# Attention in pairs of heads: scores on two row halves, weights normalised before the transpose, sums with features first, three weight buffers

## What is computed

```python
def gqa_attend(q, k, v, scale):
    s = jnp.einsum('bqhgd,bkhd->bhgqk', q, k, preferred_element_type=jnp.float32) * scale
    p = jax.nn.softmax(s, axis=-1)
    return jnp.einsum('bhgqk,bkhd->bqhgd', p.astype(v.dtype), v)
```

## Time and profile before

| | |
|---|---|
| median of 3 runs | 2904.19 us (2891.95 to 2906.38) |
| profiled execution | 2906.38 us, of it 2906.3 from first to last instruction |
| TensorE busy | 2460.7 us (85%) |
| VectorE busy | 1459.9 us (50%) |
| GpSimd busy | 934.2 us (32%) |
| ScalarE busy | 841.4 us (29%) |
| mean granted TensorE clock | 0.915 of full |

### The profile page before, as it was taken

One profiled execution on the slowest core, in us unless ns is written; L12 is line 12 of the kernel. 1 busy time (PEld: TensorE's weight loads), 2 busy tenths in 40 slices (PEclk: granted clock), 3 DMA queues, 4 the chain that ended last, 5 costly groups with the idle time before them and its releaser, 6 DMA issues. The chain is left out here.

```text
span 2906.3 us, 32667 instructions
## 1 busy us (share of the span) xinstructions
PE 2460.7 (85%) x12562; PEld 2053.4 (71%) x12562; DVE 1459.9 (50%) x2490; ACT 841.4 (29%) x1544; POOL 934.2 (32%) x572
## 2 busy tenths in 40 slices
PE   2888667988675988999689999999598997799997
PEld 2777355777354866668479998989487776588886
DVE  4776644876635956447752342222588665300112
ACT  2215113215113155443232121211412443322222
POOL 1431225320235210001354242433652001555554
PEclk9999768988777999899789999999799999899999
DMA  6540012530021310002322232332260000133222
GB/s 227 169 147 8 0 59 90 163 110 1 0 87 48 122 52 1 1 1 79 114 66 95 84 105 80 102 91 69 78 194 29 1 1 22 59 101 95 94 94 73
DMA packets 141906, 218.97 MB, mean 75 GB/s; under 512 B 12148, under 2 KB 64916, under 8 KB 141624
## 3 DMA queue, kind: packets, MB, share of 16 engines
q1 hardware_dynamic: 141752, 216.88, 23.4%
HBM read 214.75 MB, written 2.10 MB: 75 GB/s over the span
## 5 line engine op out<-in xcount | busy, mean ns | idle before, releaser
L284 POOL TENSOR_TENSOR w_lo<-w_raw,w_hi 128x1024 fp32r<-128x1024 f32 (+3 forms) x252 | 591.3, 2347 | 1306.0 <-ACT w_hi L277 1306.0
L277 ACT ACTIVATE w_hi<-w_raw 128x1024 fp32r<-128x1024 f32 (+3 forms) x252 | 255.4, 1017 | 1222.1 <-PE ps L297 986.6
L295 PE MATMUL ps<-w_hi,h_transposed 128*128 128x512 f32 (+3 forms) x1088 | 416.8, 383 | 44.2 <-DVE proj_one L678 20.8
L296 PE MATMUL ps<-w_lo,h_transposed 128*128 128x512 f32 (+3 forms) x1088 | 408.4, 375 | 0.0
L297 PE MATMUL ps<-w_hi,h_transposed 128*128 128x512 f32 (+3 forms) x1088 | 408.0, 375 | 0.0
L295 PE MATMUL ps<-h_transposed,w_hi 128*128 128x384 f32 (+1 forms) x1056 | 373.7, 354 | 3.6 <-issue 2.1
L296 PE MATMUL ps<-h_transposed,w_hi 128*128 128x384 f32 (+1 forms) x1056 | 373.2, 353 | 0.0
L297 PE MATMUL ps<-h_transposed,w_lo 128*128 128x384 f32 (+1 forms) x1056 | 373.1, 353 | 0.0
L355 DVE SCALAR_TENSOR_TENSOR mod_acc_aux<-w_raw,c_act,mod_acc_aux 128x512 f32<-128x512 f32 x280 | 275.4, 1008 | 46.4 <-DMA w_raw<-in_w_mod_dram 24.9
L295 PEld LDWEIGHTS ps<-w_hi,h_transposed 128*128 128x128 f32 x1088 | 212.7, 195 | 85.9 <-POOL w_lo L284 24.1
L1141 DVE TENSOR_TENSOR ffn_full<-ps,ffn_silu 128x768 f32<-128x768 f32 (+1 forms) x44 | 34.2, 819 | 423.6 <-PE ps L297 423.6
(11 more groups left out here) (297 smaller groups left out, 3847.8 us busy)
## 6 DMA issues: line engine op xcount, KB each, us to landing
w_raw<-in_ada_w_dram SPq DMA_DIRECT2D x96, 512.0 KB, 4.2
w_raw<-in_ffn_w_in_dram SPq DMA_DIRECT2D x88, 512.0 KB, 3.6
w_raw<-in_w_mod_dram SPq DMA_DIRECT2D x48, 512.0 KB, 4.6
w_raw<-in_ffn_w_out_dram SPq DMA_DIRECT2D x44, 512.0 KB, 3.6
w_raw<-in_w_in_dram SPq DMA_DIRECT2D x40, 512.0 KB, 4.6
w_raw<-in_w_out_dram SPq DMA_DIRECT2D x16, 512.0 KB, 4.4
w_raw<-in_od_w_in_dram SPq DMA_DIRECT2D x16, 512.0 KB, 4.6
mod_gain<-in_norm_g_dram SPq DMA_DIRECT2D x16, 256.0 KB, 4.1
```

Source lines behind the costliest of these rows:

```text
L277: act.activation(w_hi[:, i % 2, 0:k * n], w_raw[:, u % 4, 0:k * n], ACT.Copy).then_inc(w_hi_ready.sem, 1)
L284: pool.tensor_tensor(w_lo[:, i % 2, 0:k * n], w_raw[:, u % 4, 0:k * n], w_hi[:, i % 2, 0:k * n].bitcast(F32), ALU.subtract).then_inc(w_lo_ ...
L295: pe.matmul(acc, left[0], right[0], start=start, stop=False)
L296: pe.matmul(acc, left[0], right[1], start=False, stop=False)
```

## The change

Attention goes through steps, each a pair of heads.

- **Scores on two row halves.** The keys of one head lie on rows 0 to 63 and again on rows 64 to 127, with no zero halves. Each head's scores are a 64-row matmul on its half; the two heads alternate, piece by piece of the keys. The latent heads have 96 rows and stay on the whole array. The scale is now put into the queries when they are turned.
- **Weights normalised first.** VectorE forms the reciprocals right after the exponentials, and GpSimd multiplies both heads' exponentials by them in place (two TENSOR_SCALAR, L990) before TensorE transposes them. In layer one and the windowed stage GpSimd also adds the sink to the negated maximum (L982), ahead of the multiply of the step before.
- **Sums, features first.** The values are the stationary operand (64 columns) and the transposed weights move. The two heads write the two column halves of the array. The output has features on the partitions; finishing is a copy, or in layer one a product with the gate, which is now turned as well. Joined (differential) steps keep tokens first and scale at the end.
- **Transposes in rounds of four** into PSUM bank 7, a third round into bank 6, which the sums use too. Scores hold six banks. The copies are divided by round.
- **Buffers.** Three weight tiles of two heads in layer one, the windowed and the odd stage (lag 2); two in the latent stages (lag 1).
- **MixTransposed** takes parts that have features first from SBUF and transposes only the rest: nothing in the even layer, half in the others.

```diff
-            self.held, self.lag = (4, 4) if max(len(un["values"]) for un in units) <= 4 else (2, 2)
+            self.wide = max(self.blocks) > 4
+            self.slots = 3 if self.wide else 6
+            self.lag = len(probs) - 1
...
-                        for b, v in enumerate(vals):
-                            ins = pe.matmul(ps[:, 6 + o % 2, 0:v.shape[1]], self.probs_t[:, o % 2, b * P:(b + 1) * P], v,
-                                            start=(b == 0), stop=(b == len(vals) - 1))
...
+                for k in runs:
...
+                    for i in range(2):
+                        sc = self.scores(2 * s + i, w)
+                        done.append(pe.matmul(sc[:, c:c + m], x["q"][i], x["keys"][i][k][0], start=True, stop=not masks))
...
+                for b, v in enumerate(x["values"]):
+                    if self.has_join[s]:
+                        ins = pe.matmul(ps[:, self.SUM_BANK, 0:P], probs_t[:, b * P:(b + 1) * P], v, start=(b == 0), stop=(b == nb - 1))
+                    else:
+                        for i in range(2):
+                            ins = pe.matmul(ps[64 * i:64 * i + 64, self.SUM_BANK, 0:P], v[i], probs_t[:, (i * nb + b) * P:(i * nb + b + 1) * P],
+                                            start=(b == 0), stop=(b == nb - 1))
...
+                n = len(self.steps)
+                for loop in range(n + self.lag + 1):
+                    t, v = loop - self.lag, loop - self.lag - 1
+                    if loop < n:
+                        self.score(pe, loop)
+                    if 0 <= t < n:
+                        self.turn(pe, t, 0)
+                    if 0 <= v < n:
+                        self.sum(pe, v)
+                    if 0 <= t < n:
+                        for r in range(1, len(self.rounds[t])):
+                            self.turn(pe, t, r)
...
+                    s = loop - 1
+                    if s >= 0 and not self.has_join[s]:
+                        w, probs = self.width(s), self.probs[s % len(self.probs)]
+                        self.wait(pool, s_inv, s + 1)
+                        for i in range(2):
+                            r = (2 * s + i) % 16
+                            p = probs[:, i * w:(i + 1) * w]
+                            pool.tensor_scalar(p, p, st[:, 5, r:r + 1], None, ALU.mult).then_inc(s_norm.sem, 1)
...
+                self.groups = [(kt, range(tiles)) for kt in range(len(ready))]
+                self.groups += [(kt, kind) for kt in range(len(ready), KT) for kind in kinds]
```

More of the change, by code:

```diff
@@ L757, in wait_probs_ready @@
[L757 to L768, removed]
+                n = len(steps)
@@ new lines, in __init__ @@
+                self.b[s_norm], self.b[s_joined] = s_norm.plan(2 * plain), s_joined.plan(joined)
+                self.order = [sum(j == k for k in self.has_join[:s]) for s, j in enumerate(self.has_join)]
+                turned = [nb if j else 2 * nb for nb, j in zip(self.blocks, self.has_join)]
+                self.rounds = [[(i, min(4, m - i)) for i in range(0, m, 4)] for m in turned]
+                self.turn0 = [sum(len(r) for r in self.rounds[:s]) for s in range(n + 1)]
+                self.b[s_turned] = s_turned.plan(self.turn0[n])
@@ new lines, in maximum @@
+            def maximum(self, dve, s, heads):
+                u, w, m = 2 * s + heads[0], self.width(s), len(heads)
+                r = u % 16
+                self.wait(dve, s_scored, u + m)
+                if m == 2:
+                    b = u % 6
+                    src, dst = ps[:, b:b + 2, 0:w], self.st[:, 0, r:r + 2]
+                else:
+                    src, dst = self.scores(u, w), self.st[:, 0, r:r + 1]
+                ins = dve.tensor_reduce(dst, src, AX, ALU.max, negate=True)
+                sink = self.steps[s]["sink"]
+                if sink is not None:
+                    dve_s.chain(ins)
+                    h = sink + heads[0]
+                    ins = dve.tensor_tensor(dst, dst, self.neg_sinks[:, h:h + m], ALU.min)
+                ins.then_inc(s_max.sem, m)
@@ new lines, in vector @@
+            def vector(self, dve):
+                n = len(self.steps)
+                for loop in range(n + self.lag + 1):
+                    s, t, v = loop, loop - self.lag, loop - self.lag - 1
+                    if self.lag == 1 and 1 <= s <= n:
+                        self.inverse(dve, s - 1)
+                    if s < n:
+                        for heads in ([[0], [1]] if self.wide else [[0, 1]]):
+                            self.maximum(dve, s, heads)
+                    if 0 <= v < n:
+                        self.finish(dve, v)
+                    if self.lag == 2 and 1 <= s <= n:
+                        self.inverse(dve, s - 1)
+                    if 0 <= t < n:
+                        for r in range(len(self.rounds[t])):
+                            self.keep(dve, s_kept_v, t, r)
@@ L1872, in layer_even @@
-                schedule.append(Attention(units, probsb, probsb_t, stats))
-            schedule.append(MixTransposed(lambda t, kt: PE_[:, t, kt * P:(kt + 1) * P], XT + CT))
+                    blocks = list(range(XT + CT)) if t < XT else [XT, XT + 1]
+                    spans = ((0, S), (S, CTX)) if t < XT else ((S, CTX),)
+                    for j in range(2):
+                        heads = (4 * four + 2 * j, 4 * four + 2 * j + 1)
+                        steps.append(dict(q=[qbT[:, h % 4, tok(t)] for h in heads],
+                                          keys=[[(kbT[:, h % 4, c0:c0 + n], c0 if t < XT else 0) for c0, n in spans] for h in heads],
+                                          masks=[], values=[[vb[:, b, h * 64:h * 64 + 64] for h in heads] for b in blocks], sink=None, kind="plain",
+                                          dst=PE_[:, t, HALF + heads[0] * 64:HALF + heads[0] * 64 + P]))
```

469 lines of the change are left out of this document (251 added, 218 removed).

## The result

The changed kernel takes 2991.85 us (median of 4 runs, 2984.52 to 2994.54) against 2901.18 for the kernel before beside it: ratio 1.031, 95% interval 1.029 to 1.034. It is slower by 3.1%; 2836 had been forecast, and the range ended at 2885. The profiled execution has a span of 2987.5 us, 81.2 more than before.

The account below looks back on a forecast made before the run. TensorE's work was taken to set the odd stage's pace. Odd -60, windowed -19, latent 0, layer one +8 and the rest +3 gave -68: 2906.4 to 2838 profiled, 2836 as median; range 2780 to 2885.

Parts of the forecast that it names:

- The halves of the array: TensorE: two 64-row or 64-column matmuls on different halves run at once, full overlap assumed at 2.4 GHz.
- S: TensorE: price of one change of tiling, read as at most 0.19 us at half clock, taken as 0.10.
- a rival: Scores on row halves: halves keep strict order, the last pass sticks out 0.43 us per 768-wide pair; 2856, chance 0.08.
- Odd layer, -60: Odd attention stage: 8.2 us instead of 12.04 for two steps, 137 us against 197.6.
- I take 1.2: GpSimd's 768-wide multiply: 1.2 us, from 0.51 for a one-column TENSOR_SCALAR plus the fill's 0.69.
- Latent attention, 0: Both latent stages: 768-wide pairs save 8 us, 256-wide context pairs cost 7, start and end 1; no net change.
- Even layer, windowed, -19: Windowed stage: 640-wide steps save 13 us, 512-wide 10, context pairs nothing; longer start and end cost 4.
- Layer one, +4 each: Layer one's two attention stages: 47 us each against 42.6, with 2.7 us for each of 12 steps.
- Some 4.9 us over two steps, 2.4 each: Layer one: chain from exponential through reciprocal, multiplies, transposes, copy and back, spread over two steps.
- The rest, +3: Outside the attention stages: turned gates cost 2 us in each layer, MixTransposed gives -1 in all.
- The rival of dear tiling changes: Some 350 tiling changes at S = 0.40 add 105 us, so the kernel ends slower: 2941, chance 0.04.
- the first rival: Everything at TensorE's pace, multiply near the fill's price, S near 0: odd -68, windowed -27; 2779, chance 0.17.

Follow-up runs that it names:

- the VectorE run: Changed kernel with a plain step's two multiplies moved from GpSimd to VectorE, right behind the reciprocal: 2879.12 us, ratio 0.991 to the kernel before.
- The swap of two calls: Changed kernel with VectorE computing a step's reciprocals before finishing an older step, in three-buffer stages: 2932.77 us, ratio 1.009 to the kernel before.
- The edit that takes the operations apart: Changed kernel with ScalarE making MixTransposed's first four feature high parts before those of the first weights: 2982.77 us, ratio 1.027 to the kernel before.
- the short one: Changed kernel with each GpSimd multiply scaling one column only, all waits kept: 2871.12 us, ratio 0.988 to the kernel before.

## Why the prediction was wrong

Against the forecast of the profiled execution (2838) the change is 149 us late. By its own steps:

- **"The halves of the array": right.** Scores and sums of a pair overlap at 2.4 GHz. A change of tiling: in the windowed ring above the four transposes start at 1170.33 and the sums at 1170.91, 0.14 more than four passes of 0.11. The sums of the odd stage, twelve passes on each half, give the same in the VectorE run: 1.46 us to the next transposes (2327.56 to 2329.02), 0.15 more than 12 of 0.109. S is about 0.15, not 0.10: some 350 x 0.05 = 17 us where all of it is on the path. The rule of the Trainium skill that a rival rested on (TensorE: Matmul & The Clock Gate, Part 3, strict order in the queue) does not hold here: the odd scores, head by head, show passes of a free half running ahead of queued ones of the other, 1.57 us for what takes 1.56 in turns.
- **"Odd layer, -60": mis-sized, -34.** The text had "at 2.12 about 158"; with 2.20 it was 163. The failed term is "I take 1.2" for the multiply. Both of its parts were off: one column takes 0.28 us, not 0.51, and the other 767 take 1.92, not 0.69. With VectorE's 0.62 the stage is 143.5, against 137 forecast for a GpSimd at 1.2; about 5 of the 6.5 left is S (96 x 0.05).
- **"Latent attention, 0": mis-sized, +35 for both.** The same term. The ring of 6.8 us stood in the rival; it measured 6.9. With the multiply on VectorE the two stages take 66.7 and 68.5 us, against 67.9 before.
- **"Even layer, windowed, -19": the bound was wrong, +8.** The step took TensorE's work as the pace and gave GpSimd no place in it. GpSimd alone had 3.1 us a step at 512 columns, and the ring made it 4.0. With either cause taken out the stage still has 95 to 100 us for the 87 forecast; S gives 6 of it (112 x 0.05), and the rest is open.
- **"Layer one, +4 each": +28.6 and +26.6.** "Some 4.9 us over two steps, 2.4 each", for the chain through the multiplies, failed. It divided the chain by the buffers and did not walk VectorE's program order, which ties it into a ring of one step. The swap of two calls, alone, gave 24 and 20 us of it. The granted clock then fell to 0.60, which the sum did not price; it came back with the same swap.
- **"The rest, +3": +17.** "-1 in all" for MixTransposed failed, it is +18: the mechanism, VectorE's two-input subtraction alternating with GpSimd, was named, but not that the first product waits for all of it while TensorE, with fewer transposes to do, idles for 5.1 us and then starts at the lower clock. The edit that takes the operations apart gave 9 back.

How the 149 splits: stages 135, the rest 14. The multiply's length covers 121 at most, since the short one is shorter than what was forecast. The two causes overlap in layer one and the windowed stage (59 and 113 us alone, and 111 together, since the swap then holds a bank in the wide stages), so no clean division between them exists. Not settled: why layer one's clock stays low in some runs, and the last part of MixTransposed, which no run took out completely.

The estimate from the Trainium skill that stood beside the multiply's price (GPSIMD Engine Reference, section Performance versus the Vector engine) was 0.66 to 1.15 us for 768 columns; 2.20 was measured, so its figure for one-input loops does not hold for this operation. The forecast's own 1.2 came from two rows and did not rest on it. The rival "GpSimd's multiply is slow" had 0.13 and the true mechanism in part, yet even its 2880 was 112 short: it had the multiply's price, but neither the ring of one step, which the swap shows to be worth 59, nor MixTransposed. The rival of dear tiling changes came nearest in number (2941), by luck: it had S at 0.40. The 2779 of the first rival is a time of the profiled execution; as a median it is 2777.

## What to carry to other kernels

When an operation has no row on its engine, price it by the longest operation of that width there, and ask which faster engine has time: here the same multiply took 0.62 us on VectorE for 2.20 on GpSimd, and that alone turned a 3.1% loss into a 0.9% gain. When buffers are added to hide a chain, walk each engine's program order and look for an older step's operation in front of a newer one's: by the order of the two queues a third buffer does not open a ring of one step, though here it is worth 54 us once the multiply is short. The order of two short operations can be right in one stage and wrong in the next, so look at who waits for each of them.

## What was not expected of the hardware

- GpSimd's one-input multiply: 0.28 us for one column and 2.50 ns for each further one (924 ns at 256, 2205 at 768). VectorE's, from SBUF to SBUF: 350 and 618 ns, and the 618 is shorter than its 0.95 us maximum over the same 768 columns from PSUM.
- TensorE's queue looks ahead: passes on a free half overtake queued ones of the other half (all four of a 768-wide head's scores, about four of twelve in the sums, by the starts), and did not pass a matmul on the whole array in these runs.
- Layer one with scores head by head shows TensorE busy for 68.69 of 74.80 us and a granted clock of 0.53, near the lower of its two levels; the VectorE run has 35.64 of 49.70 busy at 0.88. A high busy share in that column does not go with the higher clock here. The two runs have the same 288 passes; the one with fewer of them side by side, and so with longer passes at the lower level, is the busier one.
